# Three edits to a two-layer decoder kernel: norms moved into the block of their projection, and two pieces of the RWKV merge made earlier

## The chip, the cores and the metric

The kernel runs on one core of a Trainium2 chip, as one launch. The metric is the device time of an execution in microseconds (us); the time shown is the median of three runs. A profile is one further execution, taken by the hardware profiler.

## The reference, cut to what matters

The program computes two layers of a decoder for a 512-token prompt and, beside it, eight sequences that decode one token each: T = 520 columns in all, D = 1024. Each layer does:

```
h  = rms_norm(x, norm1) * (1 + sc1) + sh1          # sc1, sh1, gt1 ... from silu(c) @ w_ada
z  = h @ w_in                                      # retention, attention, RWKV and gate columns
ya = retention(z); yb = differential_attention(z); yc = rwkv7(z)
# tail of the RWKV branch, per head of 64:
yc = (yc - mean) * rsqrt(var + eps) * lnx_g + lnx_b
yc = yc + sum(r * k * r_k) * v                     # the "bonus"
yc = yc * (sigmoid(gd) @ w_g_up)
merged = gate_a * (ya @ w_up_a) + gate_b * (yb @ w_up_b) + gate_c * (yc @ w_up_c)
x  = x + gt1 * (merged @ w_out)
h2 = rms_norm(x, norm2) * (1 + sc2) + sh2
x  = x + gt2 * (relu(h2 @ w_ff1)**2 @ w_ff2)
```

All inputs and outputs are float32.

## The kernel before

Activations are kept transposed, with the 1024 features in eight tiles of 128 partitions and the 520 tokens along the free axis (`xT`, `ht`, `yT`). A float32 matmul that carries weights is made of three: weight and activation are each split into a high part in a rounded format and the low remainder. ScalarE makes the high part by a copy (`split_hi`, L540; the activations likewise), VectorE the low one by a subtraction (`split_lo`, L548), and TensorE multiplies high x high, high x low and low x high into one PSUM bank. One such unit of work is half of a 1024 x 512 weight block (`fm_unit`, 96 matmuls of 260 columns, or the loop in `token_major`, 60 of 512). Weights come through a ring of two slots, loaded by SyncE's DMA queue (`load_w`, L525, `load_w4`, L531).

The two layers are one loop body. The body is a row of blocks (`nc.Block()`); within a block each engine runs its own written list, held together by semaphores, and at a block's end all engines meet before the next one begins. There is no scheduler: the order is the written one. The blocks that the change touches, in order:

- **Start** (L649 to L778). SyncE loads a block of `w_ada`, the first block of `w_in`, stores `x` to DRAM (`x_spill`), then loads nine small broadcast rows (four lambdas, L656; five norm rows, L658) and the second `w_in` block. TensorE makes the conditioning (`rows`, `turn`); VectorE waits for the nine rows (semaphore `loaded`), computes the lambda product (L758) and then makes, tile by tile, the normed `ht` (L770) and its low part `h_low` (L774), while ScalarE makes the high part (L715).
- **Retention projection** (`token_major`, L844): TensorE multiplies `h` with `w_in`, unit by unit.
- **Turns** (L1930): decode steps of the RWKV state on VectorE, while TensorE transposes `v`, `b` and `k` and ScalarE copies the results (L1996).
- **RWKV scan** (L2040): four chunks of 128 tokens, a ping-pong between TensorE's 64 x 64 products and VectorE's masks and sums; ScalarE copies `x` (L2220) and the outputs (L2224).
- **Merge preparation** (L2237): VectorE norms `yc` (`ytok`), scales it, adds the bonus product (L2282, L2283), multiplies by the gate product from PSUM (L2287); TensorE transposes the result head by head and VectorE copies it to `yT` (L931).
- **Merge** (L2296): six units of the three up-projections. Before the first, ScalarE and VectorE split the first `w_up_a` half (L540, L548) and the columns of `ya` (`y_hi(0)` L2322, `y_lo(0)` L2352).
- **Second norm** (`norm_stage`, L589) as a block of its own, then the **first feed-forward** (L2459, `fm_unit`). In the norm VectorE writes eight tiles of `h_low` (L618), ScalarE their high parts (L642).

## Time and profile before

| | |
|---|---|
| three runs | 3147.04, 3153.51, 3164.07 us; median 3153.51 us |
| profiled execution | 3167.52 us, span of its instructions 3165.7 us |
| busy share of the span | TensorE 86%, VectorE 47%, ScalarE 25%, GpSimd 5% |
| granted TensorE clock, mean | 0.895 of full |

The profile's views used are: groups of instructions by line (busy time, mean duration, the idle time just before them and what ended it), the timeline of one engine, and windows (busy time, granted clock and DMA share of a stretch). PE is TensorE, DVE VectorE, ACT ScalarE, SP SyncE; a trailing q (ACTq, PEq) is that engine's sequencer, so a semaphore or the meeting of all engines at a block's end.

### The profile page before, as it was taken

The page shows a single profiled execution, that of the slowest core. Times are in us where ns is not written, and L with a number is a line of the kernel's source. Part 1 is how long each engine was busy: PE and PEld are TensorE (multiplying, and loading weights), DVE is VectorE, ACT ScalarE, POOL GpSimd, SP SyncE. Part 2 cuts the span into 40 slices and gives each one's busy share as a digit, 9 for nine tenths or more (in the row PEclk, how much of TensorE's full clock was granted, in tenths as well). Part 3 has the DMA queues.
Part 4 walks back from the last instruction along what each step waited for, and adds up shares of the span by engine and source line. Part 5 has one row for each costly group of instructions (what it writes and reads, how often), then busy time and mean ns, then how long its engine had stood idle before and what let it go on. Part 6 is the DMA issues. An engine that isn't in the chain of part 4 may idle for free. (4 is left out here: it accounts for less than half of the span.)

```text
span 3165.7 us, 53418 instructions
## 1 busy us (share of the span) xinstructions
PE 2707.3 (86%) x22886; PEld 2390.5 (76%) x22886; DVE 1478.9 (47%) x2085; ACT 788.2 (25%) x1118; POOL 169.7 (5%) x102
## 2 busy tenths in 40 slices
PE   4898888987698797999959879888958969699997
PEld 2677774886587697999948768567947849699997
DVE  4234346434655755334441541744366566523343
ACT  1220214223200313233222112332241004223331
POOL 0011110300000000000000310112000000000000
PEclk9897998997598798999979979889967979899999
DMA  7212345721001341322341330656010014222223
GB/s 264 83 38 77 110 134 170 225 75 51 14 3 44 107 148 54 107 81 81 134 145 34 84 114 26 213 174 201 16 51 15 3 56 164 78 95 92 81 93 122
DMA packets 216309, 305.15 MB, mean 96 GB/s; under 512 B 28021, under 2 KB 97191, under 8 KB 214786
## 3 DMA queue, kind: packets, MB, share of 16 engines
q1 hardware_dynamic: 216066, 301.67, 28.8%
q8 instruction: 182, 2.98, 0.4%
q14 instruction: 61, 0.50, 0.0%
HBM read 266.49 MB, written 35.14 MB: 95 GB/s over the span
## 5 line engine op out<-in xcount | busy, mean ns | idle before, releaser
L373 PE MATMUL pb<-h_high,f_high 128*128 128x260 f32 x2048 | 417.3, 285 | 46.2 <-ACTq L2482 41.3
L373 PE MATMUL pb<-h_high,f_low 128*128 128x260 f32 x2048 | 415.1, 284 | 0.0
L373 PE MATMUL pb<-h_low,f_high 128*128 128x260 f32 x2048 | 414.2, 284 | 0.0
L373 PEld LDWEIGHTS pb<-h_high,f_high 128*128 128x128 f32 x2048 | 319.0, 190 | 47.3 <-issue 47.3
L548 DVE TENSOR_TENSOR w_low<-ring,w_high 128x2048 fp32r<-128x2048 f32 x64 | 146.7, 2293 | 397.6 <-ACT w_high L540 395.5
L373 PEld LDWEIGHTS pb<-h_low,f_high 128*128 128x128 f32 x2048 | 319.7, 190 | 0.0
L373 PEld LDWEIGHTS pb<-h_high,f_low 128*128 128x128 f32 x2048 | 316.9, 190 | 0.0
L548 DVE TENSOR_TENSOR f_low<-ring,f_high 128x2048 fp32r<-128x2048 f32 x64 | 146.7, 2293 | 360.2 <-ACT h_high L542 215.7
L798 POOL TENSOR_TENSOR g_low<-yT,g_high 128x512 fp32r<-128x512 f32 x96 | 167.5, 1750 | 2021.3 <-ACT g_high L794 2021.3
L373 PE MATMUL pb<-w_high,h_high 128*128 128x512 f32 x560 | 225.5, 403 | 43.4 <-ACTq L879 31.7
L373 PE MATMUL pb<-w_high,h_low 128*128 128x512 f32 x560 | 224.7, 401 | 0.0
L373 PE MATMUL pb<-w_low,h_high 128*128 128x512 f32 x560 | 224.6, 401 | 0.0
L540 ACT ACTIVATE f_high<-ring 128x2048 fp32r<-128x2048 f32 x64 | 122.7, 1917 | 376.4 <-PE pb L373 348.3
L540 ACT ACTIVATE w_high<-ring 128x2048 fp32r<-128x2048 f32 x64 | 122.3, 1917 | 363.4 <-PE pb L373 214.5
L373 PE MATMUL pb<-h_high,g_high 128*128 128x260 f32 x768 | 166.8, 300 | 43.2 <-POOL g_low L798 21.9
L373 PE MATMUL pb<-arena 64*64 64x64 f32 (+4 forms) x2320 | 185.0, 290 | 19.1 <-DVE arena L982 9.4
L373 PEld LDWEIGHTS pb<-arena 64*64 64x64 f32 (+4 forms) x2320 | 138.4, 159 | 55.2 <-issue 35.1
L373 PEld LDWEIGHTS pb<-h_high,g_high 128*128 128x128 f32 x768 | 125.0, 199 | 61.4 <-POOL g_low L798 38.0
L373 PE MATMUL pb<-h_low,g_high 128*128 128x260 f32 x768 | 160.7, 292 | 0.0
L373 PE MATMUL pb<-h_high,g_low 128*128 128x260 f32 x768 | 160.4, 292 | 0.0
L373 PEld LDWEIGHTS pb<-w_high,h_high 128*128 128x128 f32 x560 | 107.6, 192 | 69.4 <-issue 31.9
L373 PE MATMUL pb<-h_high,w_high 128*128 128x260 f32 x608 | 124.7, 287 | 11.8 <-DVEq L552 11.8
(352 smaller groups left out, 4605.3 us busy)
## 6 DMA issues: line engine op xcount, KB each, us to landing
ring<-in_w_ff_dram SPq DMA_DIRECT2D x32, 2048.0 KB, 8.0
ring<-in_w_in_dram SPq DMA_DIRECT2D x20, 2048.0 KB, 9.0
ring<-in_w_ada_dram SPq DMA_DIRECT2D x18, 2048.0 KB, 8.3
yT<-in_w_in_dram SPq DMA_DIRECT2D x96, 256.0 KB, 3.7
arena<-in_w_ada_dram SPq DMA_DIRECT2D x9, 2048.0 KB
gate_spill_dram<-yT SPq DMA_DIRECT2D x48, 260.0 KB, 4.1
arena<-gate_spill_dram SPq DMA_DIRECT2D x12, 1040.0 KB, 5.7
arena<-in_cache_k_diff_dram SPq DMA_DIRECT2D x32, 256.0 KB, 3.1
```

The lines of the kernel that those rows point to most:

```text
L373: return PE.matmul(out, lhsT, rhs, start=start, stop=stop, skip_group_check=True)
L540: t = S.activation(ws[n % 2][0], ring[slot][:, u * 2048:(u + 1) * 2048], ACT.Copy)
L548: t = V.tensor_tensor(ws[n % 2][1], ring[slot][:, u * 2048:(u + 1) * 2048], ws[n % 2][0].bitcast(F32), sub)
L798: G.tensor_tensor(g_split[j % 2][1], g_raw[j % 2], g_split[j % 2][0].bitcast(F32), sub).then_inc(gate_ready, 1)
```

## The change

What it does, part by part:

1. **Start and retention projection become one block.** The start's four lists (`start_sp`, `start_pe`, `start_s`, `start_v`) are run at the head of the projection's lists. TensorE's first unit waits for five of the eight `h_low` tiles (`h_ready`; four tiles and the next one's head are read), the second for all eight. SyncE's list loads the nine small rows first, then `w_ada`, `w_in` and the store.
2. **Second norm and first feed-forward become one block.** TensorE's first unit waits for four `h_low` tiles (`h2_ready`), its second for eight.
3. **`ya` is split earlier.** Its high part is made by ScalarE at the end of the turns block, its low part by VectorE at the head of the scan block. The two pairs of buffers for such parts change places.
4. **The bonus product moves to ScalarE in the scan**: 40 `ACTIVATE`s of 64 columns a layer, scaled per partition, 8 ahead of each chunk's copies (16 ahead of the last); they are kept in `ring`, and `rhs1` moves from there to `y_raw`.
5. **Merge preparation is rewritten.** The square goes to ScalarE; the split of the first `w_up_a` half is made here; the gate products are put in banks 4 to 7 and 0; each gated token tile is transposed at once, into banks 0 to 3; two of the four column copies go to ScalarE.
6. The merge block loses the four instructions that were made ahead.

The diff, with changes of indentation left out and cut to its core:

```diff
@@ start and second norm: the blocks become functions
-                        dv(t)
+                V.tensor_tensor(hT[1][:, k - 2], ht[:, k - 2], hT[0][:, k - 2].bitcast(F32), sub).then_inc(h2_ready, 1)
...
+            def start_sp(sp):
-                    load_w(sp, 1, L("w_ada")[:, 3 * 512:4 * 512])
-                    load_w(sp, 0, w_in[:, RET0:RET0 + 512])
-                    sp.dma_start(x_spill, x_raw).then_inc(stored, 16)
                 for i, key in enumerate(("lambda_q1", "lambda_q2", "lambda_k1", "lambda_k2")):
                     sp.dma_start(lambdas[:, i], L(key).partition_broadcast(P)).then_inc(loaded, 16)
...
+                load_w(sp, 1, L("w_ada")[:, 3 * 512:4 * 512])
+                load_w(sp, 0, w_in[:, RET0:RET0 + 512])
+                sp.dma_start(x_spill, x_raw).then_inc(stored, 16)
                 load_w(sp, 1, w_in[:, RET0 + 512:RET0 + 1024])
@@ token_major
+                        if before:
+                            before[1](pe)
                         for n in range(2 * n_blocks):
                             u = n % 2
+                            if before and n < 2:
+                                pe.wait_ge(h_ready, 3 * n + 5)
...
-            token_major(RET0, 4, 1, gates=True)
+            token_major(RET0, 4, 1, gates=True, before=(start_sp, start_pe, start_s, start_v))
@@ turns block, ScalarE
+                    S.activation(ysp[0][0], yT[:, 0:4], ACT.Copy).then_inc(y_high_ready, 1)
@@ scan block
-            rhs1 = ring[1][:, 3200:3712]
+            rhs1 = y_raw[:, 8 * T + 1024:8 * T + 1536]
...
+                    v.wait_ge(y_high_ready, 1)
+                    V.tensor_tensor(ysp[0][1], yT[:, 0:4], ysp[0][0].bitcast(F32), sub).then_inc(y_split_ready, 1)
                     dv(V.memset(stc, 0.0))
...
                     for m in range(MT):
+                        for mm_ in ((m,) if m < MT - 1 else (m, MT)):
+                            r = P if mm_ < MT else DEC
+                            for h in range(HC):
+                                S.activation(bon[0:r, mm_, h * DC:(h + 1) * DC], vtok[0:r, mm_, h * DC:(h + 1) * DC],
+                                             ACT.Identity, scale=bonus[0:r, mm_, h:h + 1]).then_inc(bonus_made, 1)
@@ merge preparation, ScalarE
+                    split_hi(s, w_split, 0, 0)
+                    s.wait_ge(dve_for_act, c["act_from_dve"].next())
+                    c["act"](S.activation(sq, ytok, ACT.Square))
...
+                    for h in (2, 3):
+                        s.wait_ge(y_turned, h - 1)
+                        S.activation(yT[:, 8 + h, 0:SEQ], pb[h], ACT.Copy)
+                        c["act"](S.activation(yT[:, 8 + h, SEQ:T], pb[4 + h][:, 0:DEC], ACT.Copy))
@@ TensorE
-                    pe_part(pe)
+                    for m in range(MT - 1):
+                        pe.wait_ge(gated, m + 2)
+                        for h in range(4):
+                            tr(pb[h][:, m * P:(m + 1) * P], ytok[:, m, h * P:(h + 1) * P])
...
@@ VectorE
-                    dv(V.tensor_tensor(sq, ytok, ytok, mult))
+                    V.sem_inc(dve_for_act, 1)
+                    split_lo(v, w_split, 0, 0)
+                    v.wait_ge(act_for_dve, c["dve_from_act"].next())
                     dv(V.tensor_reduce(ms, sg_, AX.X, add))
...
-                    dv(V.tensor_tensor(sg_, vg, bc(bonus.rearrange("p m h -> p (m h)"), [P, 40, DC], 2), mult))
-                    dv(V.tensor_tensor(ytok, ytok, sq, add))
+                    v.wait_ge(bonus_made, 5 * HC)
+                    V.tensor_tensor(ytok[:, 0:MT], ytok[:, 0:MT], bon[:, 0:MT], add)
+                    dv(V.tensor_tensor(ytok[0:DEC, MT], ytok[0:DEC, MT], bon[0:DEC, MT], add))
...
@@ merge
-                    split_hi(s, w_split, 0, 0)
-                    y_hi(0)
...
-                    split_lo(v, w_split, 0, 0)
-                    y_lo(0)
@@ first feed-forward
+                    norm_pe(pe)
                     for n in range(16):
+                        if n < 2:
+                            pe.wait_ge(h2_ready, 4 * n + 4)
```

The order of instructions at three places. Line numbers of the changed kernel differ from those of the kernel before. On SyncE, the start block, before (`arena` holds the lambdas, `rows` the norm rows, `ring` the weight slots; an ISA row sets registers; four more small rows and the second `w_in` block follow):

```order
L525 DMA ring<-in_w_ada_dram 128x8x512
L525 ISA
L525 DMA ring<-in_w_in_dram 128x8x512
L654 DMA x_spill_dram<-xT 128x4160
L656 ISA
L656 DMA arena<-in_lambda_q_dram 128x64 x2
L656 DMA arena<-in_lambda_k_dram 128x64 x2
L658 DMA rows<-in_qk_norm_q_dram 128x64
L658 DMA rows<-in_qk_norm_k_dram 128x64
L658 ISA
L658 DMA rows<-in_subln_diff_dram 128x128
```

and with the change, from the fifth small row on (the four lambdas stand ahead of it):

```order
L652 DMA rows<-in_qk_norm_q_dram 128x64
L652 DMA rows<-in_qk_norm_k_dram 128x64
L652 ISA
L652 DMA rows<-in_subln_diff_dram 128x128
L652 ISA
L652 DMA rows<-in_lnx_g_dram 128x512
L652 DMA rows<-in_lnx_b_dram 128x512
L528 ISA
L528 DMA ring<-in_w_ada_dram 128x8x512
L528 ISA
L528 DMA ring<-in_w_in_dram 128x8x512
L655 DMA x_spill_dram<-xT 128x4160
```

The nine small loads stand ahead of the two weight blocks and of the store of `x`; nothing is added or dropped.

On ScalarE, from the last copies of the turns block to the merge, before (`xT` holds `ytok` here):

```order
L2040 UNCONDITIONAL_BRANCH
L2250 UNCONDITIONAL_BRANCH
L2253 ACT_TABLE_LOAD
L2253 ACTIVATE small<-small 128x40
L2237 UNCONDITIONAL_BRANCH
L2318 UNCONDITIONAL_BRANCH
L540 ACTIVATE w_high_49<-ring 128x2048
L2322 ACTIVATE y_high<-yT 128x2080
L540 ACTIVATE w_high_51<-ring 128x2048
```

and with the change, from the scan's last chunk (the bonus products read `small` for their scale and write `ring`):

```order
L2235 ACTIVATE ring<-arena,small 128x64 x8
L2235 ACTIVATE ring<-arena,small 8x64 x8
L2239 ACTIVATE yT<-pb 128x256 x2
L2243 ACTIVATE xT<-pb 64x512 x2
L2049 UNCONDITIONAL_BRANCH
L2270 UNCONDITIONAL_BRANCH
L543 ACTIVATE w_high_49<-ring 128x2048
L2274 ACTIVATE arena<-xT 128x2560
L2277 ACT_TABLE_LOAD
L2277 ACTIVATE small<-small 128x40
L2281 ACTIVATE yT<-pb 128x512
```

The scan's last chunk gains sixteen products ahead of its copies, and the preparation gains a split, the square and four copies.

On VectorE, the merge preparation before (`xT` is `ytok`, `arena` the squares and the bonus product, `rows` the norm rows):

```order
L2273 TENSOR_TENSOR xT<-xT,small 128x2560
L2274 TENSOR_TENSOR arena<-xT 128x2560
L2275 TENSOR_REDUCE small<-arena 128x40
L2278 RECIPROCAL small<-small 128x40
L2279 TENSOR_TENSOR xT<-xT,small 128x2560
L2280 TENSOR_TENSOR xT<-xT,rows 128x2560
L2281 TENSOR_TENSOR xT<-xT,rows 128x2560
L2282 TENSOR_TENSOR arena<-arena,small 128x2560
L2283 TENSOR_TENSOR xT<-xT,arena 128x2560
L2287 TENSOR_TENSOR xT<-xT,pb 128x512 x4
L2287 TENSOR_TENSOR xT<-xT,pb 8x512
L931 COPY yT<-pb 128x512
```

and with the change:

```order
L2308 TENSOR_TENSOR xT<-xT,small 128x2560
L551 TENSOR_TENSOR w_low_50<-ring,w_high_49 128x2048
L2312 TENSOR_REDUCE small<-arena 128x40
L2315 RECIPROCAL small<-small 128x40
L2316 TENSOR_TENSOR xT<-xT,small 128x2560
L2317 TENSOR_TENSOR xT<-xT,rows 128x2560
L2318 TENSOR_TENSOR xT<-xT,rows 128x2560
L2320 TENSOR_TENSOR xT<-xT,ring 128x2048
L2321 TENSOR_TENSOR xT<-xT,ring 8x512
L2325 TENSOR_TENSOR xT<-xT,pb 8x512
L2325 TENSOR_TENSOR xT<-xT,pb 128x512 x4
L2328 COPY yT<-pb 128x512
```

The square and the bonus product have left VectorE, the split of `w_up_a` has come in between, the addition is in two pieces, and the eight-row tile is gated first.

## Rows read from the trace of the kernel before

**Rows 1.** Groups by line, shapes apart; last: idle time before, and releasers.

```profile
L373 PE MATMUL pb<-y_high,w_high 128*128 128x260 f32 x256 | 53.8, 292 | 16.5 <-DVE y_low L2352 16.5
```

**Rows 2.** Timeline of the start block, first layer: start us, us, engine, line, what.

```profile
66.78 1.91 ACT L540 ACTIVATE w_high<-ring 128x2048 fp32r<-128x2048 f32 x1 [4.76 <-DMA ring<-in_w_in_dram]
...
73.21 2.29 DVE L548 TENSOR_TENSOR w_low<-ring,w_high 128x2048 fp32r<-128x2048 f32 x1 [0.34 <-DVE yT L732]
...
81.21 0.29 DVE L758 TENSOR_TENSOR small<-arena 128x128 f32<-128x128 f32 x1 [5.71 <-DMA rows<-in_lnx_b_dram]
...
88.87 0.70 DVE L774 TENSOR_TENSOR h_low<-yT,h_high 128x520 fp32r<-128x520 f32 x1
...
93.52 0.77 PE L373 MATMUL pb<-w_high,h_high 128*128 128x512 f32 x1 [18.66 <-ACTq L879]
```

**Rows 3.** Windows: start:end and length us, busy per engine, granted clock, DMA share, GB/s.

```profile
69.00:75.00 6.00, 2.92 (x16) 1.78 (x8) 5.59 (x8) 0.99 (x1) 0.00 (x0) 0.50 0.17 49
1016.50:1053.40 36.90, 24.69 (x40) 7.71 (x40) 32.47 (x24) 1.60 (x2) 0.00 (x0) 0.52 0.24 86
2766.85:2772.10 5.25, 5.25 (x24) 5.25 (x25) 2.29 (x1) 1.81 (x1) 0.00 (x0) 0.50 0.00 0
2772.10:2778.00 5.90, 5.90 (x51) 5.90 (x50) 0.00 (x0) 0.00 (x0) 0.00 (x0) 1.00 0.91 322
```

**Rows 4.** Timeline of the start block, second layer.

```profile
1621.92 1.91 ACT L540 ACTIVATE w_high<-ring 128x2048 fp32r<-128x2048 f32 x1 [4.63 <-DVEq L746]
...
1628.48 2.29 DVE L548 TENSOR_TENSOR w_low<-ring,w_high 128x2048 fp32r<-128x2048 f32 x1 [0.34 <-DVE yT L732]
...
1638.58 0.70 DVE L774 TENSOR_TENSOR h_low<-yT,h_high 128x520 fp32r<-128x520 f32 x1
...
1643.21 0.76 PE L373 MATMUL pb<-w_high,h_high 128*128 128x512 f32 x1 [13.08 <-ACTq L879]
```

**Rows 5.** Timeline, second norm and first feed-forward matmul, both layers.

```profile
1208.13 0.69 DVE L618 TENSOR_TENSOR h_low<-arena,h_high 128x520 fp32r<-128x520 f32 x1
...
1214.31 0.77 PE L373 MATMUL pb<-h_high,f_high 128*128 128x260 f32 x2 [20.69 <-ACTq L2482]
...
2760.67 0.69 DVE L618 TENSOR_TENSOR h_low<-arena,h_high 128x520 fp32r<-128x520 f32 x1
...
2766.85 0.77 PE L373 MATMUL pb<-h_high,f_high 128*128 128x260 f32 x2 [20.56 <-ACTq L2482]
```

**Rows 6.** Timeline, end of the turns block and RWKV scan, first layer.

```profile
860.96 1.32 ACT L1996 ACTIVATE arena<-pb 128x512 f32<-128x512 f32 x2 [0.27 <-PE pb L376]
...
862.75 0.27 DVE L2147 MEMSET ring<- 128x256 f32 x1 [3.69 <-PEq L1930]
...
863.80 0.76 DVE L2153 TENSOR_TENSOR ring<-pb,cst 128x256 f32<-128x256 f32 x2 [0.77 <-PE pb L373]
...
976.66 0.38 ACT L2220 ACTIVATE yT<-pb 128x256 f32<-128x256 f32 x1 [2.02 <-PE pb L373]
...
978.57 0.36 PE L373 MATMUL pb<-yT,ring 64*64 64x64 f32 x1
```

**Rows 7.** Groups by line with shapes apart: ScalarE with a per-partition scale.

```profile
L1298 ACT ACTIVATE arena<-xT,small 128x128 f32<-128x128 f32 x16 | 6.2, 392 | 1.4 <-DVE small L1272 1.4
```

**Rows 8.** Timeline of the RWKV merge and the block behind it, first layer.

```profile
1016.52 2.82 DVE L2271 TENSOR_REDUCE small<-xT 128x40 f32<-128x2560 f32 x1 [3.62 <-PEq L2040]
...
1043.36 3.56 DVE L2287 TENSOR_TENSOR xT<-xT,pb 128x512 f32<-128x512 f32 x5
...
1047.04 5.01 PE L376 MATMUL pb<-cst,xT 128*128 128x128 f32 x20 [10.84 <-DVEq L927]
...
1053.44 1.91 ACT L540 ACTIVATE w_high<-ring 128x2048 fp32r<-128x2048 f32 x1 [24.88 <-PEq L2237]
...
1058.59 1.91 ACT L540 ACTIVATE w_high<-ring 128x2048 fp32r<-128x2048 f32 x1 [1.41 <-DMA ring<-in_w_up_a_dram]
...
1060.30 0.80 PE L373 MATMUL pb<-y_high,w_high 128*128 128x260 f32 x2 [8.25 <-DVE y_low L2352]
```

More of the change, by code:

```diff
@@ new lines, in start_pe, with rows, turn @@
+            def start_pe(pe):
+                for n in range(2):
+                    pe.sem_inc(slot_free[n], 1)
+                tr(pb[7][:, 0:NPAR], prow[0:NPAR, :]).then_inc(par_made, 1)
+                pe.wait_ge(dve_for_pe, c["pe_from_dve"].next())
+                def rows(n):
+                    w = ada_ahead[n] if n < 3 else wslot(1)
+                    for k in range(KD):
+                        cols = slice(k % 4 * 32, k % 4 * 32 + 32)
+                        t = mm(pb[n][cols, :], cs_pad[:, k, :], w[:, k, :], start=(k < 4), stop=(k >= 4))
+                    t.then_inc(pe_for_dve, 1)
+                def turn(n):
+                    pe.wait_ge(dve_for_pe, c["pe_from_dve"].next())
+                    for ct in range(4):
+                        t = mm(pb[6 + n % 2][:, ct * 9:ct * 9 + 9], mrows[:, n, ct * P:(ct + 1) * P], fold)
+                    t.then_inc(pe_for_dve, 1)
+                rows(0)
+                rows(1)
+                for k in range(0, KD, 2):
+                    pe.wait_ge(sq_made, k // 2 + 1)
+                    for half in range(2):
+                        t = mm(pb[4 + half][:, 0:TH], ones, sq[:, k, half * TH:(half + 1) * TH],
+                               start=(k == 0), stop=(k == KD - 2))
+                t.then_inc(sums_made, 1)
+                turn(0)
+                rows(2)
+                turn(1)
+                turn(2)
+                pe.wait_ge(slot_full[1], c["pe_full"][1].next(16))
+                rows(3)
+                turn(3)
@@ new lines, in start_s @@
+            def start_s(s):
+                for k in range(1, KD, 2):
+                    S.activation(sq[:, k], xT[:, k], ACT.Square).then_inc(act_for_dve, 1)
+                s.wait_ge(sums_made, 1)
+                for half in range(2):
+                    c["act"](S.activation(rstd[:, half * TH:(half + 1) * TH], pb[4 + half][:, 0:TH], ACT.Sqrt,
+                                          bias=eps, scale=1.0 / D))
+                S.sem_inc(root_made, 1)
+                s.wait_ge(dve_for_act, c["act_from_dve"].next())
+                split_hi(s, w_split, 0, 0, 0)
+                s.wait_ge(dve_for_act, c["act_from_dve"].next())
+                c["act"](S.activation(small[:, 6:8], small[:, 4:6], ACT.Exp))
+                S.sem_inc(act_for_dve, 1)
+                for k in range(KD):
+                    s.wait_ge(dve_for_act, c["act_from_dve"].next())
+                    S.activation(hT[0][:, k], ht[:, k], ACT.Copy).then_inc(act_for_dve, 1)
@@ L2213, in _ @@
                     V.sem_inc(dve_for_sp, 1)
+                bon = at(ring[1], 1536, 5, 512)
                 @block.scalar
```

304 lines of the change are left out of this document (135 added, 169 removed).

## The prediction

> **What bounds the kernel now.** I read the groups by line first, for idle time just before TensorE's matmuls. The merge loses 16.5 us to `y_low`, over both layers [rows 1], the first feed-forward 20.7 and 20.6 us behind a block boundary [rows 5]. The timelines show what TensorE waits for. In the start it begins 3.9 us after the fifth low tile was done, and in the first layer VectorE had stood 5.7 us for a small DMA [rows 2, 4]. In the second norm it begins 5.4 us after the fourth low tile [rows 5]. In the merge it begins 43.8 us after VectorE began the preparation, and between lie one long list on VectorE, a boundary, and two splits [rows 8]. Behind each of the three starts TensorE is the engine that works, so time won there should be kept. Windows show one more cost: after such a wait the granted clock is 0.50, the 1.2 GHz level, for some 5 us, 0.219 us a matmul (5.25 / 24), then 1.00 and 0.116 us (5.90 / 51) [rows 3]. A start so loses 24 x 0.103 = 2.5 us, before and after the change alike.
>
> **Second norm.** TensorE's first unit needs four low tiles: 1208.13 + 0.69 + 0.1 for the semaphore = 1208.9 against 1214.31, and 2761.5 against 2766.85 [rows 5]. That is 5.4 us a layer, **10.8 us**. The next wait is that for all eight tiles and for the second weight split; the tiles end before 1214.3 and the split takes 1.9 + 2.3 us [rows 2], so it is ready by 1217 to 1218, while the first unit needs at least 96 x 0.116 = 11.1 us [rows 3], to 1220. It is hidden.
>
> **Start.** The first unit reads five tiles: 88.87 + 0.70 + 0.1 = 89.6 against 93.52, and 1639.3 against 1643.21 [rows 2, 4]: 3.9 us a layer, **7.8 us**. The reordered loads come on top. In the first layer VectorE's wait for the nine small rows, 5.7 us up to 81.21, goes. But each of the two weight blocks is now behind them. Their shift, s, the trace does not show. Above it is 14.4 us: between `w_in` landed (66.78) and the last row (81.21), in which the rest of the store of `x` landed too [rows 2]. Below it is 0. I take 7: when the store was out, from 69 to 75 us, the DMA engines were only 17% busy and moved 49 GB/s [rows 3], so the nine go slowly, one by one, but half of the 14.4 is the store. Then `w_in` lands at 73.8, ScalarE's split ends at 75.7, VectorE's at 78.0, and the lambda product starts there instead of at 81.21: 3.2 us won. In the second layer the split on ScalarE began at 1621.92 with no DMA to wait for; 7 us later is 1628.9, plus 1.9 is 1630.8, against 1628.48 when VectorE took it up [rows 4]: at most 2.3 us lost, taken as 2.0. Net **1.2 us**. `w_ada` moves by the same s; its landing has no row, I take it to stay covered by TensorE's other work, and each us by which it is not costs one.
>
> **Turns and scan.** ScalarE's last copies end at 862.28 and the next block begins at 862.75 [rows 6]. The high part of `ya` (2080 columns, as 2048 take 1.91 us, so 1.93) is put behind them, and a block ends with its slowest engine: 1.85 us later with the overlap of neighbours. VectorE then makes the low part, 2.33 us, ahead of its memset; its first mask came 1.05 us after the block's begin, when TensorE's products were done, and can now come after 2.7 us [rows 6]. Loss 1.85 + 1.65 = 3.5 us a layer, in a ping-pong that has no slack. The 40 bonus products on ScalarE have no row. Nearest above is the 128 x 128 one with a per-partition scale, 0.392 us [rows 7]; below, all are hidden. Eight fit in the 2.02 us before the copies of `x`; sixteen ahead of the last chunk's do not. There the copies start at 974.64 + 16 p and TensorE needs the first at 978.57, 1.5 us after it was ready [rows 6]. With p = 0.28, between, it is ready at 979.5: 0.9 us late, of which the product queue takes some; I take 0.7 (ends 0 and 2.6). So **-4.2 us a layer**.
>
> The Trainium skill has a price (ScalarE: Activation LUTs, "What ACT_TABLE_LOAD costs": 186 ns + 0.833 ns a column, 93 ns more for a pointer operand, 93 ns less back to back). By it p would be an estimated 0.24 us, the delay 0.3 and the sum 0.8 us better. No run here shows it yet.
>
> **Merge preparation and merge.** Positions count from the block's begin, 1016.5 [rows 8]. Today: nine passes over 2560 elements at 2.86 us each with two short ones, gating at 26.8, its five tiles in 3.56, transposes and four copies to 36.4, boundary, at 36.9 split of weights, then of `ya`, TensorE at 43.8. With the change:
> - Mean and subtraction end at 5.9. `w_up_a` lands 5.0 us after its issue (1058.59, in a block begun at 1053.44), ScalarE splits it to 7.1 and squares to 9.4, VectorE makes the low part from 7.1 to 9.4. So the sum of squares starts at 9.6, against 8.8: the square moved away is paid by the split and 0.8 us.
> - Root, reciprocal and three passes to 21.9. The bonus is added in 2.3 + 0.6 us to 24.8; its product, 2.86 us, is gone.
> - Five gatings that no longer wait for each other, some 0.61 each, to 28.0. TensorE turns each tile at once, 1.25 us for five transposes (5.01 / 4 for the twenty of today), and ends near 30.7; VectorE and ScalarE copy two heads each, the last done at 31.9.
> - Boundary 0.5: TensorE starts at 32.5, for the split of `ya` and of the first weights is there.
>
> 43.8 - 32.5 = 11.3 us a layer. TensorE's transposes now run until 1.8 us before the merge. Before, 8.25 us of splits without a matmul lay between [rows 8], and over the preparation the clock was 0.52 [rows 3]. If it is up when the merge starts, the 2.5 us of the cold start go too, else nothing; I take half, 1.25. In the merge the next wait is the second weight half: load 5.0, splits 4.2, ready 9.3 us after TensorE's start, and the first unit takes at least 11.1. Hidden. **12.5 us a layer**, less 4.2 = 8.3, twice **16.7 us**.
>
> **Sum.** 10.8 + 7.8 + 1.2 + 16.7 = 36.5 us. The profiled execution, 3167.5 us, would become 3131; it is the slowest of what is shown, so I take the same 36.5 off the median 3153.5: **3117 us**.
>
> **Rivals.**
> - *The weights stand long behind the small rows.* With s = 14.4 [rows 2] the start of the first layer loses 4.2 us instead of winning 3.2, that of the second loses 9.4 instead of 2.0: 14.8 us less, gain 21.7, 3132 us. For it: the low DMA rate [rows 3]. Against: the store of 2 MB is in the 14.4.
> - *A new wait in the merge.* TensorE starts early, but the second half of `w_up_a` or the gate's sigmoids, which begin only with the block, come late. If the load takes 9 us instead of 5.0, unit two waits 13.3 - 11.1 = 2.2 us, and as much again if the sigmoids behind it hold the banks: 8.8 us over both layers, 3126 us. Against: the 5.0 of today's second load [rows 8].
> - *The clock (slower).* All six starts come after a shorter rest and with a wait inside the first units. Busy alone does not bring the clock back: over the preparation TensorE was 24.7 of 36.9 us busy at 0.52 [rows 3]. A unit wholly at the lower level costs 96 x 0.103 = 9.9 us; from about five such units on (36.5 + 15 already lost, over 9.9) the gain is eaten. Two at each of six starts: 12 x 9.9 - 15 = 104 us, 3221 us. Against: these same matmuls brought it back in 5.3 us [rows 3].
> - *The change does not reach the end*: time won is given back to a stage bound by DMA. Against: once the first units are in, TensorE runs without a gap at 0.116 us a matmul [rows 3]. All of it gone: 3153 us.
>
> **How the numbers follow.** Forecast 0.82, weights 0.08, merge 0.05, clock 0.03, given back 0.02. The unknowns: s from 0 to 14.4 (+4.5, -14.8), bonus (+1.4, -3.8), clock in the merge (+2.5, -2.5), so 3109 to 3138; the three runs shown lie from 6.5 below to 10.6 above their median, which a new median shares in part. Range 3102 to 3141. About 0.5%, 15.8 us, is what a measurement can tell from no change: faster is below 3138. Forecast and merge rival lie there nearly whole, the weights rival mostly: faster 0.87, within 0.10, slower 0.03.
>
> **What would show it.** Idle before the first feed-forward matmul falls from 20.7 to some 15 us; the first projection matmul follows the fifth `h_low`; VectorE shows no wait for `lnx_b`, and ScalarE's first split waits for `w_in` until about 74 us; the scan's first mask is 3.5 us later from the turns' last copy; the merge starts some 32 us after the preparation, and its first matmuls are perhaps already at 1.00. Wrong would be: a start of the second layer over 3 us later than today from the loop's begin, a first merge unit with a gap behind it, or chunks of the scan each longer by more than 1 us.

## The result, and the profile after

| | before | after |
|---|---|---|
| runs | 3147.04, 3153.51, 3153.77, 3164.07 us | 3123.76, 3126.47, 3128.06, 3128.15 us |
| median | 3153.64 us | 3127.26 us |
| profiled execution (span) | 3167.52 (3165.7) us | 3128.06 (3126.3) us |

The ratio is 0.9911, 95% interval 0.9889 to 0.9933: 26.4 us faster. (One execution of before, timed beside experiments 2, 4, 6 and 9, took 4474.08 us at a granted clock of 0.548 and is left out of every ratio and spread here.) The time forecast was 3117, the gain forecast 36.5 us. The two profiles differ by 39.4 us, which would seem to say that the forecast was nearly exact. It was not: one of its terms, the scan's, was half to three quarters of its true size, and the first pair of profiles hides that.

In the rows, a time, a duration, an engine, a line and a tile stand as in the timelines of before. In the **start of the first layer**, TensorE's first projection matmul follows the fifth low tile (87.42 + 0.69) at once, where it had waited 3.9 us [rows 2]. ScalarE's first split now waits 12.36 us for `w_in`, until 75.28, and VectorE for that split until 77.30:

```profile
75.28 1.91 ACT L543 ACTIVATE w_high<-ring 128x2048 fp32r<-128x2048 f32 x1 [12.36 <-DMA ring<-in_w_in_dram]
77.30 2.29 DVE L551 TENSOR_TENSOR w_low<-ring,w_high 128x2048 fp32r<-128x2048 f32 x1 [2.94 <-ACT w_high L543]
79.75 0.29 DVE L752 TENSOR_TENSOR small<-arena 128x128 f32<-128x128 f32 x1 [0.15 <-DVE w_low L551]
87.42 0.69 DVE L768 TENSOR_TENSOR h_low<-yT,h_high 128x520 fp32r<-128x520 f32 x1
88.16 0.79 PE L376 MATMUL pb<-w_high,h_high 128*128 128x512 f32 x1 [12.63 <-DVE h_low L768]
```

In the **second layer** ScalarE waits for `w_in` too, but VectorE comes to its low part 0.34 us behind its own list, as before [rows 4]:

```profile
1610.64 1.91 ACT L543 ACTIVATE w_high<-ring 128x2048 fp32r<-128x2048 f32 x1 [9.04 <-DMA ring<-in_w_in_dram]
1612.80 2.29 DVE L551 TENSOR_TENSOR w_low<-ring,w_high 128x2048 fp32r<-128x2048 f32 x1 [0.34 <-ACT w_high L543]
1623.65 0.80 PE L376 MATMUL pb<-w_high,h_high 128*128 128x512 f32 x1 [9.20 <-DVE h_low L768]
```

In the **second norm** the first feed-forward matmul stands 0.06 us behind the fourth low tile, 22.64 us after the block's begin instead of 27.64 [rows 5]:

```profile
1177.31 0.70 DVE L598 TENSOR_TENSOR arena<-xT 128x520 f32<-128x520 f32 x1 [0.52 <-PEq L2431]
1199.20 0.69 DVE L619 TENSOR_TENSOR h_low<-arena,h_high 128x520 fp32r<-128x520 f32 x1
1199.95 0.80 PE L376 MATMUL pb<-h_high,f_high 128*128 128x260 f32 x2 [15.38 <-DVE h_low L619]
```

In **turns and scan** ScalarE makes the high part of `ya` behind the turns' last copies, VectorE the low part ahead of its masks. The first mask comes 6.32 us after the begin of those copies instead of 2.84 [rows 6]: 3.48 us later, where 3.5 was forecast. The last chunk begins with sixteen bonus products (3.93 us, 0.246 us each), and TensorE then waits 0.89 us for the copies of `x` behind them, as it did not before [rows 6]:

```profile
859.15 1.32 ACT L2004 ACTIVATE arena<-pb 128x512 f32<-128x512 f32 x2 [0.36 <-PE pb L379]
860.59 1.94 ACT L2006 ACTIVATE h_high<-yT 128x2080 fp32r<-128x2080 f32 x1
862.84 2.33 DVE L2157 TENSOR_TENSOR h_low<-yT,h_high 128x2080 fp32r<-128x2080 f32 x1 [5.67 <-PEq L1935]
865.47 0.76 DVE L2164 TENSOR_TENSOR ring<-pb,cst 128x256 f32<-128x256 f32 x2
...
978.51 3.93 ACT L2235 ACTIVATE ring<-arena,small 128x64 f32<-128x64 f32 x16
982.46 0.66 ACT L2239 ACTIVATE yT<-pb 128x256 f32<-128x256 f32 x2
982.90 1.08 PE L376 MATMUL pb<-yT,ring 64*64 64x64 f32 x29 [0.89 <-ACT yT L2239]
```

In the **merge preparation** the merge starts 32.32 us after the block's begin instead of 43.78 [rows 8], and in the second layer the same (2549.30, 2581.62). The forecast was 32.5:

```profile
1020.13 2.82 DVE L2306 TENSOR_REDUCE small<-xT 128x40 f32<-128x2560 f32 x1 [3.61 <-PEq L2049]
1029.83 2.82 DVE L2312 TENSOR_REDUCE small<-arena 128x40 f32<-128x2560 f32 x1 [0.24 <-DVE w_low L551]
1045.07 3.07 DVE L2325 TENSOR_TENSOR xT<-xT,pb 8x512 f32<-8x512 f32 x5
1046.40 4.67 PE L379 MATMUL pb<-cst,xT 128*128 128x128 f32 x20 [6.58 <-DVE xT L2325]
1052.45 0.48 PE L376 MATMUL pb<-h_high,w_high 128*128 128x260 f32 x2 [1.39 <-DVEq L2391]
```

Two windows show the clock at the merge's first 10 us (range, length, busy time and instructions by engine, then granted clock): 64 matmuls at 0.74 before, 71 at 0.83 after.

```profile
1060.30:1070.30 10.00, 10.00 (x64) 10.00 (x65) 3.99 (x5) 7.30 (x5) 0.00 (x0) 0.74 0.23 88
```
```profile
1052.45:1062.45 10.00, 10.00 (x71) 10.00 (x72) 2.29 (x1) 4.79 (x3) 0.00 (x0) 0.83 0.60 211
```

**Positions of all stages.** Each number is the distance between two rows: VectorE's `MEMSET arena` (the start's begin), the first projection matmul, the begin of ScalarE's last two turn copies, VectorE's `TENSOR_REDUCE small<-xT` (the preparation's begin), the first merge matmul, VectorE's first square of the second norm, the first feed-forward matmul. The second column of each kernel is a second profile, from the experiments below; the last one is the kernel that came out of them.

| us | before | again | after | again | four edits |
|---|---|---|---|---|---|
| start, layer 0 | 42.01 | 42.40 | 36.53 | 36.21 | 32.57 |
| projections to turns (not touched) | 767.44 | 759.98 | 770.99 | 759.59 | 762.81 |
| turns' last copies and scan | 155.56 | 155.52 | 160.98 | 163.51 | 153.06 |
| merge preparation | 43.78 | 43.82 | 32.32 | 32.86 | 32.71 |
| second norm | 27.64 | 27.64 | 22.64 | 22.65 | 22.27 |
| start, layer 1 | 37.60 | 36.56 | 34.06 | 33.89 | 33.91 |
| projections to turns (not touched) | 770.83 | 766.15 | 764.65 | 767.90 | 764.54 |
| turns' last copies and scan | 155.57 | 155.47 | 161.00 | 163.55 | 152.29 |
| merge preparation | 43.78 | 43.84 | 32.32 | 32.72 | 32.89 |
| second norm | 27.66 | 27.64 | 22.64 | 22.65 | 22.26 |
| profiled execution's span | 3165.7 | 3151.4 | 3126.3 | 3125.3 | 3101.4 |

By the first pair the starts win 9.0 us, the preparations 22.9, the norms 10.0, and the scans lose 10.8: 31.1. By the second pair 8.9, 22.1 and 10.0 less 16.1: 24.9, near the 26.4 of the medians. Three of the four repeat; the scan is where they part.

**The scan by chunks, first layer.** From the begin of ScalarE's last two turn copies, and then from one chunk's second copy of the outputs to the next one's; in brackets, for how much of it the granted clock stood at 0.50. The numbers name experiments.

| us | before | after | again (2) | 7 | 8 | 5 |
|---|---|---|---|---|---|---|
| turn copies, chunk 1 | 40.05 (3.4) | 44.04 (10.2) | 44.02 (10.2) | 44.08 (10.2) | 44.20 (10.4) | 38.54 (0) |
| chunk 2 | 35.85 (0) | 37.35 (3.4) | 37.35 (3.4) | 37.35 (3.4) | 37.35 (3.4) | 37.16 (3.4) |
| chunk 3 | 37.18 (3.4) | 37.35 (3.4) | 37.35 (3.4) | 37.36 (3.4) | 35.85 (0) | 37.33 (3.4) |
| chunk 4 | 36.68 (3.4) | 36.45 (0) | 39.00 (6.8) | 35.17 (0) | 36.72 (3.4) | 37.00 (3.4) |

The clock falls in the scan of before too, three times for 3.4 us, once in its fourth chunk:

```profile
976.70:980.10 3.40, 3.37 (x73) 3.37 (x75) 1.41 (x5) 0.72 (x2) 0.00 (x0) 0.50 0.02 5
```

A chunk with one such fall is 1.3 to 1.5 us longer than the same chunk without (chunk 2: 37.35 and 35.85). Where it comes varies: in the second layer of before's second profile it is in the second chunk and not in the first (38.53 and 37.13 us in place of 40.05 and 35.85). So a chunk can only be compared with the same chunk at the same clock.

### The profile page after: what moved, and what is told of

Read it like the earlier page. It is cut to its first block and busy times, and to the rows that moved or that the text cites. A ratio compares the mean times of both kernels' runs of the same rounds, so it can differ in the third digit from the quotient of the medians.

```text
span 3126.3 us, 53478 instructions
## 1 busy us (share of the span) xinstructions
PE 2708.1 (87%) x22886; PEld 2389.6 (76%) x22886; DVE 1464.3 (47%) x2075; ACT 814.9 (26%) x1208; POOL 166.4 (5%) x102
## 5 line engine op out<-in xcount | busy, mean ns | idle before, releaser
L376 PE MATMUL pb<-h_high,w_high 128*128 128x260 f32 x736 | 151.9, 288 | 14.6 <-DVEq L555 11.8
L376 PE MATMUL pb<-h_low,g_high 128*128 128x260 f32 x768 | 161.0, 293 | 0.0
```

The lines of the kernel that those rows point to most:

```text
L376: return PE.matmul(out, lhsT, rhs, start=start, stop=stop, skip_group_check=True)
```

## The experiments

Each kernel was profiled once and timed in five rounds beside the kernel before. A gain against before is given by its ratio, a change against after by the positions above, since the times of one kernel spread over up to 20 us.

**1. Before, again.** No edit.

> The kernel before, unchanged, profiled a second time. Matmul for matmul, the first profile of before (3167.5 us) and that of after (3128.1) differ by 39.4 us, of which 34.5 arise in the eight stretches that the change touches, while the medians differ by 26.4 only. Theory A (the untouched stretches vary from execution to execution): time near 3150, and against the first profile the difference lies in stretches that the change does not touch (gates, attention, the second halves of the feed-forward), the starts, the scans, the merge preparations and the second norms agreeing within 0.5 us each. Theory B (the stalls that the change removes are themselves shorter in a usual execution): the same time near 3150, but the stretch from the preparation's begin to the merge's first matmul is under 42 us instead of 43.8, or the gap from the fourth low tile of the second norm to the first feed-forward matmul under 4.5 us instead of 5.4.

3155.60 us (ratio 1.0003, 0.9990 to 1.0016). Theory A holds in the main: preparation 43.82 and norm 27.64 as in the first profile, turns and scan within 0.1 us, but the untouched first stretch 7.5 us shorter, 4.7 in the second layer. The start of the second layer is 1.0 us shorter as well (36.56 against 37.60), more than the 0.5 us allowed. The runs of before spread from 3144.9 to 3164.2. Where a part of that comes from shows in the retention's gates, in which GpSimd makes low parts of 512 columns while VectorE passes over 2560. In after's first profile GpSimd's instruction began 0.06 us behind a VectorE pass with two inputs, and two such parts took 7.72 us; TensorE waited 3.15 us for the first:

```profile
438.20 2.82 DVE L1168 TENSOR_TENSOR arena<-arena,rows 128x2560 f32<-128x2560 f32 x1
438.26 7.72 POOL L791 TENSOR_TENSOR g_low<-yT,g_high 128x512 fp32r<-128x512 f32 x2 [2.83 <-ACT g_high L787]
441.06 3.77 DVE L1091 TENSOR_TENSOR arena<-arena 128x2560 f32<-128x2560 f32 x1
442.20 0.56 PE L376 MATMUL pb<-h_high,g_high 128*128 128x260 f32 x2 [3.15 <-POOL g_low L791]
```

In the second profile of before the third low part, the first of those two, began 0.5 us before a pass of VectorE ended, came in between two passes and took 1.66 us; the next pass took 3.79 instead of 2.82:

```profile
438.31 2.82 DVE L1092 TENSOR_TENSOR arena<-arena,small 128x2560 f32<-128x2560 f32 x1
440.62 1.66 POOL L798 TENSOR_TENSOR g_low<-yT,g_high 128x512 fp32r<-128x512 f32 x1 [2.22 <-ACT g_high L794]
441.16 3.79 DVE L1163 TENSOR_TENSOR arena<-arena,rows 128x2560 f32<-128x2560 f32 x1
442.33 0.51 PE L373 MATMUL pb<-h_high,g_high 128*128 128x260 f32 x2 [0.31 <-POOL g_low L798]
```

The Trainium skill says so (SBUF — State Buffer, section "SBUF: two separate sides": between VectorE with two inputs in that memory and GpSimd, whichever starts first has the shared ports for its whole instruction), and these rows agree. Against the same pass of VectorE (the one that reads `rows`), GpSimd's part began 0.06 us too late in the one profile and 0.54 us early in the other.

**2. After, again.** No edit.

> The kernel after, unchanged, profiled a second time. Theory (the 8 us between the sum of the changed stretches, 34.5, and the difference of the medians, 26.4, is the luck of two stretches with gates, where GpSimd's low parts and VectorE's passes over 2560 elements run beside each other, and not a cost of the change): with enough runs after spreads by some 10 us like before, its gates and attention of the first layer are in some executions 7 to 11 us shorter than in its first profile, and the changed stretches repeat within 0.5 us. Rival (the change makes these stretches longer, since it starts the layer earlier against the loads): the second profile shows the same long first gates, and the times stay within 3124 to 3128.

3134.07 us (ratio 0.9939, 0.9921 to 0.9957; runs 3127.0 to 3135.6). The theory holds by half. The untouched first stretch is 11.4 us shorter than in the first profile, near before's second one; that of the second layer is 3.3 us longer (767.90 against 764.64). But not all changed stretches repeat: each scan is 2.5 us longer still. In the profiles of after, of its repetition and of experiments 3, 4 and 9, which all have the same scan, six of ten scans take 163.5 us and four 161.0. All of this difference is in the fourth chunk. So the 8 us that were missing between profile and medians were in good part a cost of the change, in the scan.

**3. Small rows behind the store, as before.**

```diff
-  small rows; w_ada; w_in; store of x
+  w_ada; w_in; store of x; small rows
```

> The kernel after, with the nine small rows issued behind the store of x, as before. Theory (the order is worth little): the lambda product of the first layer stands at 81 us instead of 79.75, the first projection matmul 1.4 us later than after's; in the second layer 0.3 us earlier, since the split no longer waits for w_in. Sum 1.1 us slower: 3128 us against 3127. Rival (the order is what won the second layer's 5.0 us in place of my 1.9): the second layer's start is 3 us longer than after's, 3131 us or more.

3130.73 us (ratio 0.9921, 0.9902 to 0.9941). Starts 36.54 and 34.09, against 36.53 and 34.06: the order alone is worth nothing, in neither layer. With the old order VectorE's wait of 3.16 us for `lnx_b` is back and the lambda product stands 28.14 us after the start's begin; in after it stands at 28.12, held by the weights. Both my +3.2 and my -2.0 were wrong. The rest of the first layer's 5.5 us (3.9 by the block boundary) is that the rows landed 1.6 us earlier here than in before (29.70, and 30.10 in its second profile); why, no run shows.

**4. Small rows between the weights and the store.**

```diff
-  small rows; w_ada; w_in; store of x
+  w_ada; w_in; small rows; store of x
```

> The kernel after, with the nine small rows issued behind the two weight blocks and ahead of the store of x. Theory (on the queue, what is issued first lands first): w_in lands as early as before, ScalarE's split of it starts near 67 us instead of 75.28, VectorE's lambda product stands at 75.6 instead of 79.75, and the first projection matmul comes 4.1 us earlier than after's in the first layer and 0.3 us earlier in the second: 4.4 us, 3123 us by the first runs of after. Rival (the rows are then late: they land some time behind the weights and hold VectorE as in the kernel before): the lambda product waits for them until 77 to 78 us, and 2 us or less are won in the first layer.

Start of the first layer 32.96 instead of 36.53, of the second 33.94: 3.6 and 0.1 us won, near the theory. Neither ScalarE nor VectorE waits for a transfer now:

```profile
65.49 1.92 ACT L543 ACTIVATE w_high<-ring 128x2048 fp32r<-128x2048 f32 x1 [4.64 <-DVEq L740]
72.05 2.29 DVE L551 TENSOR_TENSOR w_low<-ring,w_high 128x2048 fp32r<-128x2048 f32 x1 [0.34 <-DVE yT L726]
74.49 0.29 DVE L752 TENSOR_TENSOR small<-arena 128x128 f32<-128x128 f32 x1 [0.15 <-DVE w_low L551]
82.90 0.79 PE L376 MATMUL pb<-w_high,h_high 128*128 128x512 f32 x1 [10.02 <-DVE h_low L768]
```

The time, 3130.22 us (0.9927, 0.9907 to 0.9947), is 3.9 us under that of experiment 2, beside which it ran; its runs spread over 12 us, so the position carries the verdict.

**5. `ya`'s parts beside the scan.**

```diff
-  (turns, ScalarE)      ysp high = copy of yT[:, 0:4]
-  (scan, VectorE)       ysp low, ahead of the memset
+  (scan, ScalarE)       ysp high, behind the first chunk's copies of x
+  (scan, GpSimd)        ysp low
```

> The kernel after, with the high part of ya made by ScalarE behind its two copies of the first chunk, and the low part by GpSimd, instead of ahead of the scan on ScalarE and VectorE. Theory (the two parts are the whole loss of the scan): the scan's begin and first chunk win back 4.1 us a layer, and the 1.4 us that the second chunk lost, while the granted clock stood at 0.5 there, perhaps too: 8 to 11 us, 3117 to 3119 us. Rival 1 (the 40 bonus products on ScalarE delay the scan): only part comes back, below 6 us in all. Rival 2 (GpSimd's subtraction of 2080 columns, some 7 us by its 1.716 us for 512, slows VectorE while both run): the first chunk gets longer by up to 3 us a layer and the gain is 2 to 4 us.

3120.33 us (ratio 0.9887, 0.9868 to 0.9905). Turns and scan 155.81 and 155.80, 5.2 us less than in after's first profile and only 0.25 more than before, with the bonus products still ahead of the copies. The theory holds in the main. Rival 1 and rival 2 fell, but the products are not free: the fourth chunk, with the clock at 0.50 for 3.4 us as in before, takes 37.00 us against 36.68. GpSimd took 4.61 us, less than estimated, and VectorE's masks beside it kept their 0.38 us each.

```profile
857.34 4.61 POOL L2247 TENSOR_TENSOR h_low<-yT,h_high 128x2080 fp32r<-128x2080 f32 x1 [230.97 <-ACT h_high L2237]
```

**6. The bonus product back on VectorE.**

```diff
-  40 products on ScalarE in the scan
+  tensor_tensor(bon, vtok, bonus), 4 tiles and the decode rows, in the preparation
```

> The kernel after, with the bonus product made again by VectorE in the merge preparation (over 4 tiles and the decode rows) and not by ScalarE during the scan. Theory (the 40 products on ScalarE cost the scan nothing, the product on VectorE 2.3 + 0.6 us of the list that sets the merge's start): the preparation gets 2.9 us longer a layer, the scan keeps its length, 5.8 us slower than after. Rival (the products delay the scan by the 1.5 us seen in its second chunk): the second chunk wins back 1.5 us a layer, and the sum is 2.8 us slower than after.

3134.54 us (ratio 0.9932, 0.9912 to 0.9953). Preparation 35.96 and 35.91 against 32.3 to 32.9: 3.1 to 3.6 us longer, a bit over the 2.9 of theory. But turns and scan take 159.73 and 159.70, 1.3 or 3.8 less than in after's two profiles, all of it in the fourth chunk. So the products ahead of the copies do cost the scan something, against the theory, and not in the second chunk, against the rival; where, the next experiment shows.

**7. The bonus products behind the copies of `x`.**

```diff
   for m in range(MT):
-      8 or 16 bonus products
       2 copies of x
+      8 or 16 bonus products
       2 copies of the outputs
```

> The kernel after, with one edit: in each chunk of the scan ScalarE makes the bonus products behind the two copies of x instead of ahead of them, where it then waits some 24 us anyway. With the products on VectorE the fourth chunk up to its second level was 1.24 us shorter than in the first profile of after (35.86 against 37.12 us) and 2.4 us shorter than in three others, in which the granted clock stood at 0.50 for 6.8 us there. Theory (the sixteen products ahead of the last copies make all of that): the fourth chunk gets 1.24 us shorter a layer and the drop of the clock to 0.50 for 6.8 us is not seen: 2.5 us in all against the first profile of after, up to 7.5 against the second, a time of 3125 to 3130 us. Rival (VectorE's product took 2.9 us out of the preparation and the clock's drop fell elsewhere by chance): the fourth chunk is as long as after's, 37.1 us or more, and the time that of after.

3123.73 us (ratio 0.9903, 0.9885 to 0.9921). Turns and scan 159.75 and 159.74: 1.25 us under after's first profile, 3.8 under its second. The theory holds in place and size: the fourth chunk takes 35.17 us against 36.45 and 39.00, and the clock stays up in it. In after's second profile the clock stands at 0.50 for 6.8 us, in which 125 matmuls are done; with the copies first, 206 are done in 5.8 us at 1.00:

```profile
971.61 1.86 PE L376 MATMUL pb<-yT,ring 64*64 64x64 f32 x29 [0.80 <-ACT yT L2239]
```
```profile
970.50:977.30 6.80, 6.00 (x125) 5.81 (x123) 2.99 (x8) 1.31 (x5) 0.00 (x0) 0.50 0.01 2
```
```profile
972.20:978.00 5.80, 5.70 (x206) 5.57 (x207) 4.47 (x13) 4.56 (x18) 0.00 (x0) 1.00 0.01 3
```

So the products ahead of the copies cost 1.25 us where the clock stays up, and the fall of the clock 2.5 more. That the wait brings the clock down is not shown: it fell at 970.50, 0.3 us before the wait for the copies began (970.81), and after's first profile has a like wait, 0.89 us, without a fall. TensorE's rest of 1.92 us ahead of it, at the head of the chunk, is there in before and in experiments 6 and 7 alike, and the clock falls behind it in the first and not in the others. What decides is open.

**8. The state's store in the next block.** The store's issue and its wait move from the scan block's end to the preparation, behind the load of `w_up_a`.

> The kernel after, with the store of the scan's state issued and waited for at the head of the next block, behind the load of w_up_a, instead of at the scan block's end, where every engine stood 3.4 to 3.6 us for it (VectorE's last copy 1016.09 to 1016.5, preparation's begin 1020.13). Theory (that store alone holds the block): the preparation begins 0.5 us behind VectorE's last copy, 3.1 us earlier a layer, and the list on VectorE keeps its length: 6.2 us, 3121 us. Rival (the time comes back as a wait for w_up_a or for the gates, which now share the queue with the store): VectorE waits before its low part of w_up_a for more than today's 1.3 us, or ScalarE for the gates in the merge, and the gain is under 3 us.

3124.70 us (ratio 0.9909, 0.9887 to 0.9930). The preparation begins 0.44 us behind VectorE's last copy instead of 3.61, and its list keeps its length:

```profile
1010.80 2.82 DVE L2303 TENSOR_REDUCE small<-xT 128x40 f32<-128x2560 f32 x1 [0.44 <-PEq L2049]
1043.57 0.77 PE L376 MATMUL pb<-h_high,w_high 128*128 128x260 f32 x2 [1.39 <-DVEq L2388]
```

3.2 us are won at the head of the list, and the positions of all later stages are those of after's second profile (merge 32.77, norm 22.64). Against after's first profile, in which the merge's first matmuls were faster, 1.9 us a layer are left at the same matmul some 20 us on. The theory is right in place and, at a merge that starts cold, in size.

But turns and scan take 156.73 us in both layers, 4.25 less than in after's first profile and 6.8 less than in its second, and only 3.2 of that is the store's. The rest goes with the clock: it does not fall in the third chunk, and in the fourth it falls for 3.4 us (table above). With sixteen products ahead of the same copies, TensorE does not wait for them there, since at the lower clock it is still busy when they land, and the chunk takes 36.72 us, as in before:

```profile
973.70:977.10 3.40, 3.40 (x72) 3.25 (x70) 1.50 (x5) 2.96 (x12) 0.00 (x0) 0.50 0.00 0
```
```profile
976.03 0.66 ACT L2239 ACTIVATE yT<-pb 128x256 f32<-128x256 f32 x2
976.47 1.36 PE L376 MATMUL pb<-yT,ring 64*64 64x64 f32 x30
```

So what the products cost is 1.25 us with the clock up, 0 to 0.3 (experiments 8 and 5) with a fall of 3.4 us that before has as well, and 2.3 to 3.8 with one of 6.8 us, counted from before and from experiment 7.

**9. Unread matmuls against the cold start.** 28 ahead of the transposes, 14 ahead of the feed-forward.

> The kernel after, with 28 matmuls of 260 columns more on TensorE ahead of the transposes of the merge preparation (while it waits for VectorE's gating) and 14 ahead of the first feed-forward unit (between the first and the fourth low tile); their results are overwritten unread. Theory (what is lost at a start is the rest before it, at any work): the granted clock is up when the merge and the feed-forward begin, their first matmuls take 0.116 us instead of 0.219; at the feed-forward 1.5 to 1.9 us are won a layer, at the merge 1 to 2.1 us, and the transposes get shorter: 5 to 8 us in all. Rival (the clock does not rise for such short work before a gap of 1 us): the first units take as long as after's, and the 42 matmuls cost nothing or, where they run into the gated tiles, up to 1 us a layer.

3128.21 us (ratio 0.9920, 0.9898 to 0.9942). Theory and rival each hold in a part. The transposes run in 3.51 us instead of 4.67, the merge starts 31.33 and 31.16 us after the preparation's begin, and the merge of the second layer is at 1.00 from its first matmul (83 in 10 us, against 71). In the first layer the merge is hardly faster than in after's first profile (72 matmuls at 0.86 against 71 at 0.83). In the feed-forward nothing is won: the 14 end 2 us too early, and the first 10 us of the first layer hold 62 matmuls at 0.71, where after has 69 at 0.81.

```profile
1046.80 3.51 PE L379 MATMUL pb<-cst,xT 128*128 128x128 f32 x20 [1.22 <-DVE xT L2327]
```
```profile
2581.53:2591.53 10.00, 10.00 (x83) 10.00 (x84) 1.62 (x1) 3.54 (x3) 0.00 (x0) 1.00 0.59 211
1199.00:1209.00 10.00, 10.00 (x62) 10.00 (x63) 6.98 (x9) 3.09 (x4) 0.00 (x0) 0.71 0.07 15
```

**10. Four edits together** (4, 5, 7 and 8).

> The kernel after with four edits: small rows between weights and store (4.2 us measured over both layers), ya's parts beside the scan (3.4 us of a layer kept at its end), bonus products behind the copies of x, the state's store in the next block (1.9 us a layer kept). Theory (they add up, since each shortens another stretch): 4.2 + 2 x (5.3 + 1.2) + 2 x 1.9 = 21 us under after, 3108 us by the runs of after near 3129. Rival (the drops of the clock, which moved by one or two us with each edit, take back what the scan wins): 10 us or less, 3119 us or more.

3106.72 us (ratio 0.9854, 0.9836 to 0.9872), 46 us under before and 20 to 27 under after, whose two medians are 3127.3 and 3134.1. The edits add up, as the last column of the table of positions shows: start 32.57, turns and scan 153.06 and 152.29 (3.2 of the gain is the store's), preparation and norm as in after. It is the simplest of the three fastest kernels.

**11. Unread matmuls up to each start, on the four edits.**

> The kernel of the four edits, with unread matmuls that run up to each start without a gap: 30 ahead of the transposes of the merge preparation, 12 sums and 15 matmuls on the first three low tiles ahead of the first feed-forward unit, 20 on the first four low tiles ahead of the first projection. With 14 and then a gap of 2.4 us the feed-forward had still begun at 0.50 for 5.7 us, while the merge of the second layer began at 1.00 and kept it. Theory (what counts is that TensorE works up to the start): the first units at 1.00, 2 us won at each of two projections, two merges and two feed-forwards, 8 to 12 us under the kernel of the four edits. Rival (the clock answers later than 5 us, or the extra matmuls delay the first unit): no start is more than 1 us shorter and the time is that of the four edits.

3103.81 us (0.9837, 0.9821 to 0.9854). Only the projections answer, elsewhere the rival holds: their first 10 us hold 43 matmuls at 1.00 against 33 at 0.74 in the first layer, 42 against 37 in the second. Merge and feed-forward begin as before (62 against 63, 69 against 71). The difference to the four edits, 2.9 us, lies within the spread of either.

**12. The low part of `w_up_a` on GpSimd, on the four edits.**

> The kernel of the four edits, with the low part of the first half of w_up_a made by GpSimd in the merge preparation instead of by VectorE, whose list there sets the merge's start. Theory A (GpSimd works beside VectorE): the list loses 2.29 us and a short wait, the merge starts 2.3 to 2.7 us earlier a layer. Theory B (the two exclude each other, as in the gates, where GpSimd's 1.29 us became up to 4.4 and VectorE's pass of 2.83 became 3.78): VectorE's passes beside it get 1 us longer, 1.3 us are won a layer, and GpSimd takes 4.6 us or more. Rival: the low part is late for the merge and TensorE waits.

3105.51 us (0.9841, 0.9824 to 0.9858), preparation 32.71 and 32.77: nothing won. Neither theory: GpSimd's 4.53 us ran undisturbed, but VectorE then waited 3.79 us for ScalarE, whose split and square now end last:

```profile
1016.63 4.53 POOL L2273 TENSOR_TENSOR w_low<-ring,w_high 128x2048 fp32r<-128x2048 f32 x1 [146.77 <-ACT w_high L543]
1018.86 2.82 DVE L2319 TENSOR_REDUCE small<-arena 128x40 f32<-128x2560 f32 x1 [3.79 <-ACTq L2283]
```

## Why the prediction was right, and where it was not

The sign, the places and most sizes were right: faster, by the mechanisms named, and 3127.26 lies in the range. That the first pair of profiles comes within 3 us of the 36.5 forecast is luck.

- **Second norm, 10.8 us.** 10.0 in both pairs. The handoff is 0.06 us where 0.1 was assumed; the tiles themselves come 0.4 us later in the block.
- **Start, 7.8 + 1.2 us.** 9.0 and 8.9, but the parts differ: the boundaries gave what was said, the reordered loads nothing (experiment 3), and that 1.2 is right is luck: the rows landed earlier than in before with either order. The shift of the weights was 8.5 us (66.78 to 75.28), near the 7 taken; what it gave and took was mis-sized: 0 where +3.2 and -2.0 were said. That the weights do come later behind the rows these runs show; that nothing lets them pass, as the prediction has it, is more than they show.
- **Merge preparation, 11.3 us a layer.** 11.46 in the first pair, 11.0 and 11.1 in the second. The listed positions hold: sum of squares at 9.7 (9.6), gating's end at 28.0 (28.0), the transposes' end at 30.9 (30.7). Experiment 6 prices the product taken off the list at 3.1 to 3.6 us, and 12 shows that behind the split in VectorE's list stands ScalarE's square.
- **Clock at the merge, 1.25 us a layer.** Some 0.8 in the first profile (71 matmuls instead of 64, at 0.116 us each), 0.1 in the second (65). It is no gain to count on. "Before and after the change alike" was wrong in the other direction elsewhere: the first 10 us of the feed-forward hold 69 matmuls at 0.81 in both layers, against 65 and 63 at 0.76 and 0.74 before.
- **Turns and scan, -4.2 us a layer: the step that failed.** Measured -5.4 in the first profile and -8.0 in the second, which is the commoner. The 3.5 us for the parts of `ya` were right where they were worked out, at the first mask (3.48). The step that failed is what was left out behind it: the sum counts waits at one clock, and puts the granted clock inside the scan at nothing, although it falls there in before too. Behind the parts of `ya` it stands at 0.50 for 10.2 us of the first chunk instead of 3.4, and for 3.4 us of the second, where before has no fall; with them it is 4.0 us more to the end of the first chunk and 1.5 us more in the second. The bonus delay, "I take 0.7", was 1.25 with the clock up, and 3.8 with a fall of 6.8 us, against the same kernel with the copies first (experiments 2, 6, 7). The product's own duration was 0.25 us, not the 0.28 taken; TensorE's wait was 0.89, the 0.9 foreseen. (The Trainium skill's estimate of 0.24 by ScalarE: Activation LUTs, "What ACT_TABLE_LOAD costs", agrees with the 0.246 measured; the delay of 0.3 that was worked out from it does not.) So the next thought, that the product queue takes some of that wait, was wrong where the clock stays up; the upper end named, 2.6, was too low because of the clock. The two costs do not add: with the parts of `ya` gone, the clock falls elsewhere, and the bonus ahead of the copies costs 0.3 (experiment 5). How long the clock is at 0.50 in each chunk the profiles show; why it falls in one chunk or execution and not in another they do not.

By the second pair of profiles the terms come to 10.0 + 8.9 + 22.1 - 16.1 and 0.2 by the clock at the merge, 25.1 us; the medians gave 26.4. Of the 11.4 us that are missing to 36.5, 7.7 are the scan, 2.3 the clock, 0.8 the norms, 0.5 the preparations and 0.1 the starts. The 39.4 us of the first pair are 31.1 in the table's changed rows, 2.6 in its untouched ones and 5.7 in the stretches from the first merge matmul to the second norm (2.5) and from the first feed-forward matmul on (3.4), less 0.1 ahead of the first start. How often the scan takes 161.0 and how often 163.5 us in the executions that were only timed isn't known.

The rivals: the weights' long shift, 14.4, did not come (8.5). No new wait arose in the merge. The clock did not slow the starts; it cost time in another place, the scan.

## What to carry to other kernels

Work that is off the critical path in one stage is not free in the stage that it is moved to: in a ping-pong between two engines put it behind the copy that the other engine needs, not ahead of it, or on an engine that takes no part. Compare such a stretch piece by piece, with the granted clock of each piece beside it: the same edit cost 0, 1.25 or 3.8 us here by where the clock fell. Before a gain is read from one pair of profiles, profile each kernel twice and compare the stretches that the change doesn't touch. And look at each block's end for a transfer that is only waited for there because it was issued there.

## What was not expected of the hardware

- The granted clock falls to 0.50 inside the scan of every kernel here: three times for 3.4 us in before, and for up to 10.2 us of a chunk in after. A fall of 3.4 us makes a chunk 1.3 to 1.5 us longer, and where it comes varies between executions of one kernel.
- GpSimd's subtraction of 512 columns takes 1.3 us alone, and two of them 7.72 beside VectorE's passes with two inputs, while 2080 columns took 4.61 beside VectorE's short masks. A part that came 0.06 us too late kept TensorE waiting for 3.15 us, one that came 0.54 us early for 0.31.
- A per-partition scaled `ACTIVATE` of 64 columns takes 0.246 to 0.252 us in a row of its kind.
